# Another order of blocks, steps and plain sets in the two-half MLP of a hybrid backbone layer

## The reference

```python
D_MODEL = 1024; SEQ = 2048; D_FF = 4 * D_MODEL

def sq_relu_mlp(h, w1, w2):
    return jnp.square(jax.nn.relu(h @ w1)) @ w2
...
        x = x + mod[:, :, 5] * sq_relu_mlp(modulate(x, norm2_g[l], mod, 3), mlp_w1[l], mlp_w2[l])
...
    return rmsnorm(x, final_g)
```

## Time and profile before

| | us |
|---|---|
| median of three runs | 2624.35 |
| profiled execution | 2627.44 |
| its span on the core | 2625.6 |
| TensorE busy | 2459.6 (94%) |
| VectorE busy | 1745.2 (66%) |
| ScalarE busy | 1051.4 (40%) |
| GpSimd busy | 601.5 (23%) |

### The profile page before, as it was taken

One profiled execution on the slowest core, in us unless ns is written; L12 is line 12 of the kernel. 1 busy time (PEld: TensorE's weight loads), 2 busy tenths in 40 slices (PEclk: granted clock), 3 DMA queues, 4 the chain that ended last, 5 costly groups with the idle time before them and its releaser, 6 DMA issues.

```text
span 2625.6 us, 39469 instructions
## 1 busy us (share of the span) xinstructions
PE 2459.6 (94%) x14636; PEld 1352.1 (51%) x14636; DVE 1745.2 (66%) x3086; ACT 1051.4 (40%) x2078; POOL 601.5 (23%) x511
## 2 busy tenths in 40 slices
PE   7888989998899999989996899999999999999997
PEld 2445646554667868676443344444444444444443
DVE  6860545578768656556577888888896655556575
ACT  3844444367543423333454444444423322222212
POOL 0408545100000000021235443444341000000020
PEclk9999999999999999999998999999999999999999
DMA  7404323000100000140344445444528533333322
GB/s 234 130 18 140 101 85 93 18 25 9 28 19 24 12 18 18 34 113 17 90 167 142 159 164 177 141 152 152 173 85 290 187 102 99 105 104 101 98 76 65
DMA packets 176455, 260.26 MB, mean 99 GB/s; under 512 B 21320, under 2 KB 90952, under 8 KB 175608
## 3 DMA queue, kind: packets, MB, share of 16 engines
q1 hardware_dynamic: 171656, 240.95, 29.3%
q0 software_dynamic: 4608, 16.78, 2.0%
HBM read 179.18 MB, written 78.50 MB: 98 GB/s over the span
## 4 chain that ended last, share of the span: by engine, by line
PE 58%; issue 15%; DVE 13%; ACT 7%; POOL 3%; DMA 2%; SPq 1%; ACTq 0%; DVEq 0%; POOLq 0%
PE pb L2949 17%; PE pb L3048 13%; PE pb L329 11%; PE pb L2934 3%; PE pb L3063 2%; DVE arena L2459 2%; DVE arena L2375 2%; PE pb L2884 2%; POOL MS L1714 1%; PE pb L2561 1%; PE pb L338 1%; DVE arena L2277 1%; PE pb L295 1%; PE pb L2766 1%; DVE arena L2284 1%
## 5 line engine op out<-in xcount | busy, mean ns | idle before, releaser
L2949 PE MATMUL pb<-arena 128*128 128x512 f16 (+2 forms) x2760 | 594.5, 377 | 31.1 <-DVE arena L2423 18.3
L3048 PE MATMUL pb<-arena 128*128 128x512 f16 x2352 | 514.6, 379 | 5.0 <-DVE arena L2459 3.7
L2949 PEld LDWEIGHTS pb<-arena 128*128 128x128 f16 x2760 | 268.5, 99 | 352.4 <-DVE arena L2277 26.8
L329 PE MATMUL pb<-arena 128*128 128x512 f16 (+1 forms) x1944 | 412.9, 374 | 13.3 <-DVE arena L1918 4.5
L3048 PEld LDWEIGHTS pb<-arena 128*128 128x128 f16 x2352 | 228.5, 98 | 286.8 <-DVE arena L2459 15.7
L2459 DVE SCALAR_TENSOR_TENSOR arena<-pb,arena 128x512 f32<-128x512 f32 x432 | 293.3, 686 | 47.1 <-PE pb L3048 24.3
L329 PEld LDWEIGHTS pb<-arena 128*128 128x128 f16 x1944 | 191.3, 99 | 232.8 <-issue 20.1
L1543 ACT ACTIVATE pb<-pb 128x512 f32<-128x512 f32 x192 | 111.8, 583 | 202.4 <-DVE pb L2430 97.4
L338 PE MATMUL pb<-arena 128*128 128x128 f16 x2880 | 173.1, 221 | 6.8 <-ACT arena L1314 4.9
L338 PEld LDWEIGHTS pb<-arena 128*128 128x128 f16 x2880 | 168.1, 99 | 9.5 <-ACT arena L1314 5.1
L1778 POOL TENSOR_TENSOR arena<-arena 128x512 f32<-128x512 f32 x8 | 13.4, 1699 | 501.9 <-DVE arena L2459 501.9
(11 more groups left out here) (359 smaller groups left out, 3876.5 us busy)
## 6 DMA issues: line engine op xcount, KB each, us to landing
w1x<-arena SPq DMA_DIRECT2D x112, 256.0 KB, 2.1
arena<-w1x SPq DMA_DIRECT2D x112, 256.0 KB, 2.7
w2x<-arena SPq DMA_DIRECT2D x106, 256.0 KB, 2.1
arena<-w2x SPq DMA_DIRECT2D x106, 256.0 KB, 2.9
arena<-in_x SPq DMA_DIRECT2D x128, 128.0 KB, 3.7
arena<-in_ada_rest POOLq DMA_DIRECT2D x32, 512.0 KB, 3.9
arena<-in_mlp_w SPq DMA_DIRECT2D x64, 256.0 KB, 6.2
arena<-in_mlp_w SPq DMA_DIRECT2D x16, 1024.0 KB, 5.6
```

The lines of the kernel that those rows point to most:

```text
L329: mm = pe.matmul(pb[:, bank(jb, b), 0:n], whl[:, (i + 1) % 2, KT * ws + k, :], hT[:, k, hs, t0:t0 + n], start=(k == 0 and m == 0), stop=(k ...
L2949: mm = pe.matmul(pb[:, up_bank(pas, s, j), c], (lo if ws else hi)[:, k, :], token_op(b, L // 2, c)[:, k, hs, :], start=(k == 0 and m == 0) ...
L3048: mm = pe.matmul(pb[:, 4 + at % 4, :], left[:, hs, P * tt:P * tt + P], right[:, ws, :], start=(e == 0 and m == 0), stop=(e == 1 and m == 2))
```

## The change

`steps()` becomes `phases()`, one list over both halves. Sets 0 and 1 are the plain ones (`PLAIN = 2`), sets 2 to 15 are paired to steps 0 to 6. In the first half the order is U(0), U(1), plain 0, U(2), plain 1, U(3), and then each step follows its second set: products at positions 0 to 2, the next block, positions 3 to 6, the next block. The second half starts with set 2 and has its plain sets at the end; its blocks U(2) and U(3) stand inside and behind the first half's last step. The operands that are quadrants (0, 1, 2) are copied and subtracted inside the block, the four others behind the evictions of the next part. U uses one set of banks for all sets but the first. There are 15 slots each for hidden operands and second weights. Token blocks are fetched back one at a time, the first half's final norm moves into the second half's U(3) and first step, and set 0's weights are written out in two groups, four of them before the kernel waits for `x_park`.

```diff
-            return (BANKS_HIGH if s == 1 else BANKS_LOW)[j]
+            return BANKS_LOW[j]
...
-        LASTQ = (0, 5, 4, 3, 2, 1, 6)
...
+        LASTQ = (0, 2, 1, 5, 4, 3, 6)
+
+        def step_order(pas, p):
+
+            return LASTQ if p == NSTEP - 1 else (0, 4, 5, 1, 2, 3, 6) if pas and p == 0 else range(7)
...
+        def phases():
+
+            out = [(0, "U", 0, ()), (0, "U", 1, ()), (0, "C", 0, ()), (0, "U", 2, ()), (0, "C", 1, ()), (0, "U", 3, ())]
             for pas in range(2):
                 for p in range(NSTEP):
+                    more = p < NSTEP - 1
+                    out += [(pas, "D", p, (0, 1, 2)), (pas if more else 1, "U", 2 * p + 4 if more else 0 if pas else 2, ()),
+                            (pas, "D", p, (3, 4, 5, 6)), (pas if more else 1, "U", 2 * p + 5 if more else 1 if pas else 3, ())]
+            return out + [(1, "C", 0, ()), (1, "C", 1, ())]
...
-        def steps():
-
-            out = [("U", 0, ()), ("U", 1, ())]
-            for p in range(NSTEP - 1):
-                out += [("U", 2 * p + 2, ()), ("D", p, (0, 1, 2, 3)), ("U", 2 * p + 3, ()), ("D", p, (4, 5, 6))]
-            out += [("U", STRASSEN, ()), ("D", NSTEP - 1, tuple(range(7))), ("U", NSET - 1, ())]
-            return out + [("C", STRASSEN, ()), ("C", NSET - 1, ())]
...
+        A_SUMS = {(0, 1): 0, (0, 3): 1, (1, 1): 2, (1, 3): 3, (3, 1): 0, (3, 3): 1, (4, 1): 2, (4, 3): 3}
+        A_LO = {(0, 2): 3, (1, 0): 4, (1, 2): 5, (2, 0): 6, (3, 2): 3, (4, 0): 4, (4, 2): 5, (5, 0): 6}
+        A_SUMS_SOON, A_LO_SOON = {(0, i): i for i in range(4)}, {(0, i): 3 + i for i in range(4)}
...
             load_w1(1)
+            for op in WSEQ0[0:4]:
+                keep_w1(0, op)
             sp.wait_ge(*late("x_park", 16))
...
+            def following(products):
+                for j in products:
+                    fetch_tokens(PRODUCTS[j][1])
+                    fetch_w1(SETS[1][0], PRODUCTS[j][0])
```

In ScalarE's and VectorE's code for a block (`act_up`, `dve_up`), the lines that the change adds inside:

```diff
                 squared(pas, s, "A11", 0)
+                a_hi(pas, s, 0)
...
+                if (pas, s) == (1, 3):
+                    final_sq(0, range(4))
                 squared(pas, s, "A22", 1)
+                a_hi(pas, s, a_order(s)[1])
...
                 squared(pas, s, "A12", 2)
+                a_hi(pas, s, 1)
+                if (pas, s) == (1, 3):
+                    final_sq(0, range(4, 8))
...
                 dve.tensor_tensor(TS, T0, bank(2), ALU.add).then_inc(S("u_c"), 1)
+                a_lo(pas, s, 0)
...
+                if (pas, s) == (1, 3):
+                    final_out(0, 0)
...
+                a_lo(pas, s, a_order(s)[1])
...
+                a_lo(pas, s, 1)
                 dve.wait_ge(S("u_mm"), up_done(pas, s, 6))
```

In the first step of the second half, and for the banks of U:

```diff
+                            if q == 0 and tt == 0 and pas:
+                                dve.wait_ge(*late("comb", 12))
+                                dve.wait_ge(*late("comb_d", 16))
+                                dve.wait_ge(S("h_sq"), N7 + 8)
...
+                    if pas and p == 0 and pos in (0, 2):
+                        final_out(0, 2 + pos // 2)
...
+                elif j == 0:
+                    pe.wait_ge(S("u_c"), uc(*prior, "A21"))
```

More of the change, by code:

```diff
@@ new lines, in _ @@
+            for pas, what, i, qs in phases():
+                if what == "U":
+                    act_up(pas, i)
+                elif (pas, what, i) == (1, "C", 1):
+                    final_sq(1, range(8))
+                else:
+                    s = rest_set(pas, what, i, qs)
+                    w2 = VSEQ if (pas, what, i) == (0, "C", 1) else ()
+                    for q in w2[0:2]:
+                        w2_hi(2, q)
+                    for k in a_order(s[1])[3:]:
+                        a_hi(*s, k)
+                    for q in w2[2:7]:
+                        w2_hi(2, q)
@@ L2541, in dve_plain @@
                     final_out(pas, 3)
[L2543 to L2550 removed]
+            for pas, what, i, qs in phases():
+                if what == "U":
+                    dve_up(pas, i)
+                elif what == "D":
+                    dve_step(pas, i, qs)
+                else:
+                    dve_plain(pas, i)
         @block.tensor
```

515 lines of the change are left out of this document (267 added, 248 removed).

## The result

The changed kernel takes 2672.3 us (2669.7 to 2673.1, 4 runs), the kernel before 2624.8 (2623.2 to 2625.5, 4 runs): ratio on record 1.0174, 95% interval 1.0161 to 1.0187 (the two medians alone give 1.018). It is slower, as forecast, but by 47 us where 20 were forecast. The profiled execution took 2671.5 with a span of 2669.6, 44.0 above the span of before.

The account below looks back on a forecast made before the run. TensorE was taken to bound the kernel, with every matmul kept, so only its waits could change: -15.8 (start) + 27.1 (steady first half) + 8.8 (seam) = +20.1, profiled 2647.5, forecast 2644.4 us, own range 2628 to 2660.

Parts of the forecast that it names:

- Steady first half: Parts behind sets 3 to 14 lose 34.8 us in all against 7.7 before: +27.1 us.
- I take 2.9 us per part: Each first-half part behind sets 3 to 14: 2.5 us wait before the fifth bank, 0.4 at the twelfth.
- the 3.0 of the sum: Copies and differences added to the chain at a block's end make the first eviction 3.0 us later.
- 2.0 us of the start: Loss in the second plain set, where VectorE has 31 operations in 20.7 us and two meet GpSimd.
- Rival 2: Clock falls at the first half's waits, a further 2.2 us each, 26 in all: 2671 us; chance 0.12.
- Start: Start loses 17.3 us against 33.1 (13.0 first wait, 2.3 cold clock, 2.0 second plain set): -15.8 us.
- hardly a gain: At the start, ScalarE's first weight copy running 9 us earlier hardly helps, since GpSimd's 4.64 us scaling remains the obstacle.
- Rival 3: Start doesn't shrink, as set 2 waits as much as set 1's 13 us: 2660 us; chance 0.10.
- Seam: Between the halves, 7.4 us removed, 16.2 added by last-step joins, final row norms and clock: +8.8 us.
- the larger loss that the prediction weighed for the last step: Last four-product part: joins could each wait up to a GpSimd add, losing more than the forecast 2.7 us.
- Rival 1: Steady first half: added copies fit into the chain's gaps, parts lose 0.6 us as today: 2612 us; chance 0.22.
- Second half and tail: Second half loses nothing, as A12 and A21 follow their products at once; tail is the same work.

Follow-up runs that it names:

- experiment 2: Changed kernel with the low part of A11 made behind U4's add instead of ahead of the sum GpSimd waits for: 2656.1 us, ratio 1.0109.
- experiments 1 and 3: Changed kernel: 1, TensorE also waits for the A12 add at first-half parts' heads, 2660.7 us; 3, four operations moved within the chain, 2626.6 us.
- experiment 5: Changed kernel with GpSimd's sums for first-product operands 4 and 6 made ahead of its first second-product weight scaling: 2668.3 us, ratio 1.0166.
- experiment 9: Changed kernel with the writes of set 0's seven first-product weight operands back at their old place on SyncE's queue: 2677.9 us, ratio 1.0184.
- experiment 6: Chain-reordered kernel (2626.6 us) with the seam's last four norm squares behind ScalarE's copies and all norm products out of the block: 2628.6 us, ratio 1.0011.
- experiment 7: Chain-reordered kernel (2626.6 us) with low parts of the seventh first- and second-product weight operands behind the step's first two evictions: 2632.5 us, ratio 1.0024.
- experiment 4: Changed kernel with GpSimd's difference of tokens made one set later: 2668.9 us, ratio 1.0152.
- experiment 8: Changed kernel with chain reordered, token difference later, GpSimd's sums earlier, two low parts behind evictions, norms behind the second half's first products: 2630.7 us, ratio 1.0019.
- experiment 10: Chain-reordered kernel (2626.6 us) with GpSimd's token difference one set later and its sums ahead of its first scaling: 2624.8 us, ratio 0.9992.

## Why the prediction was right in direction and wrong in size

- **Steady first half, +27.1 forecast, +49.0 measured.** This is the step that failed: "I take 2.9 us per part". The wait itself was right: eleven parts have 2.74 (one 3.02), with the resumption 2.9 each, its releaser and place as forecast. The first eviction came 3.1 us later than before, against the 3.0 of the sum, and experiment 2 confirms the price of one operation. That the part's 2.9 was met so exactly is in part luck: 0.4 of it was to be lost at the twelfth bank, where there is no wait, and the wait at the fifth is longer than the 2.5. Two things were not in the sum: the clock, which fell behind nine of the eleven (15.1 us), and the first part, which cost 9.5 instead of 2.9 (6.6). 27.1 + 15.1 + 6.6 = 48.8. The second is mostly GpSimd's scaling of weights, which in this one part falls beside the low parts ahead of the first eviction, and 1.1 us of VectorE's lateness out of the second plain set. I had put a meeting with GpSimd only later in the part, and had priced the lateness as 2.0 us of the start, where TensorE waited 0.50 and 0.36.
- **Rival 2** was half of the truth, and I had treated it as an alternative where it was an addition: it needs the forecast's wait to exist. The evidence was there: 0.62 and 1.30 without loss, 4.72 and more with it; 2.5 lay between, and I gave it 0.12. Its 2671 is close to the measured time by luck: it has 26 of clock (12 waits at 2.2) where 15.1 came (nine at 1.69 or a little less), and knows nothing of the first part. The Trainium skill (TensorE: Matmul & The Clock Gate, "HAM oscillation — how this bites in real kernels") has it that repeated waits between bursts pay the warm-up each time; the trace agrees for nine of eleven waits of 2.7 to 3.0 us, and in experiments 1 and 3 the rows behind waits of 0.3 to 1.94 lost 0.25 us at most.
- **Start, -15.8 forecast, -14.7 measured.** First wait 13.94 instead of 13.0, ended by the A21 add; GpSimd's scaling decided (experiment 5), but the early writes were worth more than "hardly a gain" (experiment 9). Rival 3 is out: no wait at set 2.
- **Seam, +8.8 forecast, +8.3 measured.** The wait before the second product is 8.35 against 8.3; the next 1.08 against 3.8; the clock took 2.9 (x24 in 8.24 instead of 5.34) against 1.4; the last step's joins cost three waits of 0.24, 1.09 and 0.58 against 2.7. Experiment 6 confirms the norms as the cause. The Trainium skill (SBUF — State Buffer, "Who interferes with whom") has it that a VectorE operation with two SBUF inputs contends with a GpSimd operation that reads SBUF. The trace agrees in single rows (in the last step a low part of 1.43 and joins of 0.84 and 0.85 beside GpSimd's adds of 1.27; 2.83 in experiment 7), but the larger loss that the prediction weighed for the last step didn't come: its three waits are 1.9 in all, not over 2.7.
- **Rival 1** is out: the gaps in the chain grew with it.
- Second half and tail: 0.2 against 0.
- No load was late in the second half's first block.

Open stays why two of eleven nearly equal waits kept the clock in this kernel, four in experiment 4, and two in 9. No run told that apart, and with one trace for each kernel it isn't known whether the number also varies from one execution to the next.

## What to carry to other kernels

When work is pulled forward so that one product follows at once on another, list what stands ahead of the first buffer release, on every engine of the chain. Put the added operations where their engine waits anyway, and not between one engine's result and the other engine that needs it: here that order was worth 41 us at equal work, with nothing moved behind the release. Moving two operations behind it (experiment 7) delayed a load, and cost more than it gave. A wait has two prices, its length and the clock behind it; where many equal waits of 2 to 3 us are forecast, add the second, and if they can't be removed, cut them in two. And work out the first part of a stage by itself: here other engines' work fell elsewhere than in the parts that follow, and it cost three times as much as an ordinary one was forecast to.

## What the runs showed of the hardware that I had not expected

- A single wait of 2.7 to 3.0 us took TensorE to its lower clock in most cases (nine of eleven) at 1.69 us each; waits of 2.13 in two of nine; a wait of 1.66 (once 1.94) and one of 0.89 with 5.35 us of matmuls between them in none of ten parts. At the seam a wait of 2.40 lost it in experiment 6, and one of 2.39 in experiment 8 did not.
- Moving GpSimd's work out of VectorE's way moved other GpSimd work into it: 2.58 became 0.69, another row 1.16 became 2.23 (experiment 4). In experiment 7 a load issued 1.2 us later lengthened such a meeting from at most 1.55 to 2.85 us. Low parts with an input in PSUM (L2460) took 0.67 to 0.69 us throughout, in these kernels and in the changed one.
- Behind a long wait the price in clock has no order that the runs show: the x84 row behind the first wait, 18.29 at full clock, took 20.33 after 10.60 us, 20.98 after 10.71, 19.76 after 12.67, 21.11 after 13.82 and 20.96 after 17.71. So of the 3.0 us less waiting in experiment 10, 2.3 went to a slower clock without the runs saying why.
